# Empty expert slots left out of the gathers and stores of a mixture-of-experts block

## The chip, the cores and the metric

The kernel runs on one core of a Trainium2 chip. The metric is the device time of one execution in microseconds; the kernel before was timed in three runs.

## The reference

Two transformer blocks follow each other for 512 tokens of width 1024, in float32. The first has differential and latent attention, a cross attention to 256 memory tokens, and a mixture of 32 experts in 4 groups; the second has a gated delta rule, sliding-window attention and two feed-forwards. The change concerns the mixture alone, which for each token h is

```
g = top-1 group of softmax(h Wg + bg);  e1, e2 = top-2 experts of that group by softmax(h We + be)
w_k = p(g) * p(e_k) / (p(e1) + p(e2))
y = sum over k of w_k * (silu(h G[e_k]) * (h U[e_k])) D[e_k]      G, U: 1024 x 256,  D: 256 x 1024
```

The reference pads each expert's tokens to blocks and fills the rest with an empty token of weight 0.

## The kernel before

**Blocks and slots.** The kernel gives each expert a block of 64 slots (`SLOTS`). Experts 0 to 30 are the static blocks (`N_STATIC` = 31); expert 31, and what an expert has beyond 64 tokens, go into extra blocks, run by a loop whose count is read from the router's result. The router (`router_vector`, on DVE, with rank sums on PE) gives each of the 1024 pairs of token and choice a slot (`DEST`), and by a product of one-hot tables (`ids_tensor`) each slot its token (`IDS`). An empty slot gets the sum of nothing, token 0. A token's slots within a block are filled from slot 0 up.

**Rows in.** SP stores the tokens' rows (1028 floats with the norm's factor) to `rows_h` in DRAM. POOL gathers 128 of them for a pair of blocks by an indirect DMA (`gather`, L2269; the last pair and the extra block have 64), two buffers deep (`XB`); before the gather of pair q it waits until PE has turned pair q-2. DVE scales them, PE turns them (`turn_x`), DVE puts them into `XT` with the gain.

**Weights.** SP loads each block's weights as three pieces of 1 MB (`load_piece`, L1962, `load_extra`, L1976) into a ring of 16 places (`RING_X`) that borrow other tensors' memory. `queue` is their order, the order in which PE uses them; a piece is loaded when the piece 16 before it is done.

**Work.** `macros` is the order on PE, ACT and DVE: gate and up of block b (`gate_up`, L2011 and L2013), `down` of b-1 (L2022), the turn of b's hidden (L2097). The extra loop stands after down of block 23 (`X_AT` = 24), its result goes to buffer 0. In the first blocks and ahead of them PE also makes the second layer's memory keys (L2041).

**Rows out.** ACT copies the result [2 halves x 64 slots, 512] from PSUM to `YB` (in `scratch`, one buffer per parity, L2203) and itself issues two stores of 128 KB (`store_y`, L1984) to `rows_y`, which has a row for each slot; before it overwrites a buffer it waits for the stores of two blocks ago (`y_stored`). Slots of extra blocks that aren't run are filled with constants once, by a 4 MB DMA from POOL (L3527, `st_fill`).

**Combination.** When all stores have landed, POOL gathers for each of the four token tiles both choices' rows by slot (8 indirect DMAs, L2297). DVE adds them with their weights to `ROWS` (L2399), PE turns the sums back (L2357) and makes the beta products (L2342), ACT copies them to X, POOL multiplies by the final gain's row (L2304). SP meanwhile loads gdnin tiles of the second layer: six once the last pieces leave their places (`first_tiles`), the others as tiles are split.

## Time and profile before

| | |
|---|---|
| Median of three runs | 2062.88 us (2062.76 to 2064.25) |
| Span of the profiled execution | 2062.3 us |
| PE busy | 1919.4 us, 93% |
| DVE, ACT, POOL busy | 51%, 38%, 6% |
| DMA over the span | 261.07 MB, mean 127 GB/s |
| Expert stage, first gather to last gate and up | 463 to 726 us |

The profiled execution is told by its span alone; its own device time wasn't recorded, and the median stands 0.6 us above the span. A line of the trace names a place in the code (L2022), an engine and what it writes and reads by the program's names; PE is the matrix engine, PEld its weight load, SPq, ACTq and POOLq are the queues that issue DMAs. "<-" ahead of a name tells whose end released an instruction. The chain of waits is followed back from the last instruction. Each slice of the page is a fortieth of the span, 51.6 us.

### The profile page before, as it was taken

Reading aid. Unit: us, or ns where it says so; the run is one execution under the profiler, and the core shown is the slowest. Engines: PE = TensorE matmul, PEld = TensorE weight load, DVE = VectorE, ACT = ScalarE, POOL = GpSimd, SP = SyncE. Lnnn points to the kernel's source line nnn. Section 1 sums busy time; section 2 is a strip of 40 time slices with the busy share of each in tenths; the row PEclk is TensorE's granted clock in tenths of the full one; section 3 lists DMA queues with packets and bytes.
Section 4 is the critical chain, followed back from the end, with each engine's and each line's share of the span. In section 5 each row is a group of like instructions: output and inputs, shape, how many; then the busy total and the mean of one; then the engine's idle time right before and its main releaser. Section 6 shows DMA issues by size and latency. Waiting matters only on the chain.

```text
span 2062.3 us, 25543 instructions
## 1 busy us (share of the span) xinstructions
PE 1919.4 (93%) x9978; PEld 1494.5 (72%) x9978; DVE 1059.4 (51%) x1979; ACT 779.8 (38%) x1637; POOL 117.1 (6%) x85
## 2 busy tenths in 40 slices
PE   7999888998987759999898999999999999999997
PEld 5665567685544447788887888888876778888886
DVE  6757656352211147684554543644567754444344
ACT  4455744531111146533544331322345543222222
POOL 0000000000000034020420000000000000000000
PEclk9999989999999969999999999999999999999998
DMA  5101513449999951122001222222221022222221
GB/s 188 42 10 38 161 53 109 148 180 406 412 412 408 405 226 62 62 72 72 1 2 46 97 98 102 87 98 99 95 82 42 32 100 95 102 92 92 102 92 41
DMA packets 76792, 261.07 MB, mean 127 GB/s; under 512 B 7777, under 2 KB 10081, under 8 KB 76289
## 3 DMA queue, kind: packets, MB, share of 16 engines
q1 hardware_dynamic: 66512, 231.46, 30.7%
q0 software_dynamic: 5040, 19.58, 2.8%
q10 hardware_dynamic: 5120, 8.39, 1.1%
q8 instruction: 80, 1.31, 0.3%
q14 instruction: 40, 0.32, 0.1%
HBM read 242.62 MB, written 16.79 MB: 126 GB/s over the span
## 4 chain that ended last, share of the span: by engine, by line
PE 72%; DMA 7%; DVE 6%; ACT 3%; issue 1%; POOL 0%; SPq 0%; ACTq 0%; DVEq 0%; POOLq 0%
PE ps_pair L299 17%; PE ps_pair L300 17%; PE ps_pair L301 17%; PE ps_pair L2011 3%; DMA w_places<-w_experts 3%; DMA split_acts_as_f<-w_experts 3%; PE ps_turn L2576 2%; PE ps_pair L2576 1%; PE ps_pair L892 1%; PE ps_out L923 1%; PE ps_out L2022 1%; PE ps_turn L904 1%; PE ps_shared L2022 1%; PE ps_out L2342 1%; ACT g L3368 1%
## 5 line engine op out<-in xcount | busy, mean ns | idle before, releaser
L299 PE MATMUL ps_pair<-split_acts,w_high 128*128 128x512 f32 (+1 forms) x1816 | 723.2, 398 | 21.8 <-DVE split_acts L626 10.0
L301 PE MATMUL ps_pair<-split_acts,w_low 128*128 128x512 f32 (+1 forms) x1816 | 706.0, 389 | 0.0
L300 PE MATMUL ps_pair<-split_acts,w_high 128*128 128x512 f32 (+1 forms) x1800 | 700.0, 389 | 0.0
L299 PEld LDWEIGHTS ps_pair<-split_acts,w_high 128*128 128x128 f32 x1816 | 344.7, 190 | 103.2 <-issue 23.7
L242 DVE TENSOR_TENSOR w_low<-w_raw,w_high 128x1024 fp32r<-128x1024 f32 (+4 forms) x249 | 281.9, 1133 | 259.8 <-ACT w_high L236 257.8
L301 PEld LDWEIGHTS ps_pair<-split_acts,w_low 128*128 128x128 f32 x1816 | 344.2, 190 | 72.1
L300 PEld LDWEIGHTS ps_pair<-split_acts,w_high 128*128 128x128 f32 x1800 | 342.5, 190 | 67.6 <-issue 1.9
L236 ACT ACTIVATE w_high<-w_raw 128x1024 fp32r<-128x1024 f32 (+4 forms) x249 | 242.8, 976 | 147.2 <-PE ps_pair L301 143.2
L372 DVE TENSOR_TENSOR x<-x,ps_pair 128x512 f32<-128x512 f32 x80 | 54.9, 686 | 141.5 <-PE ps_pair L301 141.5
L2253 DVE TENSOR_TENSOR g<-g,ps_pair 64x256 f32<-64x256 f32 x31 | 13.2, 425 | 199.7 <-ACT g L2193 199.7
L3124 ACT ACTIVATE split_acts<-h 128x512 fp32r<-128x512 f32 x44 | 27.9, 633 | 200.2 <-DVE h L3137 200.2
L3119 ACT ACTIVATE h<-h 128x512 f32<-128x512 f32 x44 | 27.8, 632 | 138.4 <-DVE h L3130 138.3
L2011 PE MATMUL ps_pair<-split_acts_as_f 128*64 128x256 f32 x232 | 62.6, 426 | 16.4 <-DMA split_acts_as_f<-w_experts 10.8
L957 ACT ACTIVATE g<-ps_pair,columns 128x256 f32<-128x256 f32 (+3 forms) x112 | 57.4, 524 | 35.8 <-DVE columns L1011 33.9
L3134 DVE TENSOR_TENSOR h<-ps_pair,h 128x512 f32<-128x512 f32 x44 | 30.4, 691 | 78.5 <-PE ps_pair L301 78.5
L2013 PE MATMUL ps_pair<-split_acts_as_f 128*64 128x256 f32 x232 | 62.9, 427 | 0.0
L3130 DVE TENSOR_TENSOR h<-ps_pair,h 128x512 f32<-128x512 f32 x44 | 30.4, 691 | 58.9 <-PE ps_pair L301 53.2
L2576 PE MATMUL ps_turn<-split_acts_as_f 128*128 128x128 f32 x432 | 55.8, 280 | 3.9 <-ACT split_acts_as_f L2723 3.9
L2011 PEld LDWEIGHTS ps_pair<-split_acts_as_f 128*64 128x64 f32 x232 | 34.5, 153 | 33.4 <-issue 19.7
L2707 POOL TENSOR_TENSOR split_acts_as_f<-split_acts_as_f,consts 128x768 f32<-128x768 f32 x24 | 45.2, 1894 | 226.7 <-DVE split_acts_as_f L2692 131.5
L2576 PEld LDWEIGHTS ps_turn<-split_acts_as_f 128*128 128x128 f32 x432 | 52.9, 196 | 5.8 <-issue 5.0
L2193 ACT ACTIVATE g<-ps_pair 64x256 f32<-64x256 f32 x31 | 11.6, 375 | 120.0 <-PE ps_pair L2013 120.0
(528 smaller groups left out, 2459.1 us busy)
## 6 DMA issues: line engine op xcount, KB each, us to landing
w_raw<-w_gu SPq DMA_DIRECT2D x88, 512.0 KB, 3.4
split_acts_as_f<-w_experts SPq DMA_DIRECT2D x42, 1024.0 KB, 21.2
w_places<-w_experts SPq DMA_DIRECT2D x35, 1024.0 KB, 21.4
w_raw<-w_down SPq DMA_DIRECT2D x32, 448.0 KB, 3.2
w_raw<-w_gdnin SPq DMA_DIRECT2D x26, 512.0 KB, 3.4
w_raw<-w_out SPq DMA_DIRECT2D x24, 512.0 KB, 3.5
x<-w_experts SPq DMA_DIRECT2D x12, 1024.0 KB, 20.0
rows_y<-scratch ACTq DMA_DIRECT2D x64, 128.0 KB, 6.1
```

Source lines behind the costliest of these rows:

```text
L236: act.activation(WH[:, t % SPLIT, 0:kt * m], WRAW[:, t % RING, 0:kt * m], ACT.Copy).then_inc(high_ready, 1)
L242: dve.tensor_tensor(WL[:, t % SPLIT, 0:kt * m], WRAW[:, t % RING, 0:kt * m], WH[:, t % SPLIT, 0:kt * m].bitcast(F32), ALU.subtract).then_i ...
L299: pe.matmul(out, wh[:, k, :], self.high(k), start=(n == 0), stop=False)
L300: pe.matmul(out, wh[:, k, :], self.low(k), start=False, stop=False)
L301: last = pe.matmul(out, wl[:, k, :], self.high(k), start=False, stop=(n == self.kt - 1))
L372: dve.tensor_tensor(X[:, j, :], X[:, j, :], out, ALU.add).then_inc(evacuated[t % BANKS], 1)
L957: done(act.activation(self.member(self.prob(n), j, w), self.member(self.bank(m), j, w), ACT.Exp, bias=COL[:, c + j:c + j + 1], scale=self. ...
L2011: pe.matmul(out[rows, 0:256], xs, w[:, at_:at_ + 256], start=(k == 0), stop=(k == KT - 1), skip_group_check=True)
L2013: last = pe.matmul(out[high_rows, 0:256], xs, w[:, at_ + 256:at_ + 512], start=(k == 0), stop=(k == KT - 1), skip_group_check=True)
L2022: last = pe.matmul(out[n * SLOTS:(n + 1) * SLOTS, :], h[:, k * SLOTS:(k + 1) * SLOTS], w[:, k * 1024 + n * 512:k * 1024 + n * 512 + 512], ...
L2576: last = pe.matmul(pair(bank)[:, n, :], lhs(h), rhs(h), start=True, stop=True)
L2707: done(pool.tensor_tensor(CM[c], LT[c], wide(level(l)), ALU.mult), "c_pool", ("C", c, l))
```

## The change

Empty slots get indices out of bounds, and the indirect DMAs get a bound and skip them. Each slot's list entry now is 2 x token + choice - 1024 before the sum, so a filled slot gives 2 x token + choice, and an empty one 1024 (`OF_SLOT`); halved it is the token, or 512 where empty (`IDS`), and doubled plus the half (`HALF_ROWS`) it is the place of a half row of 512 floats in `rows_y`. `rows_y` shrinks from a row for each slot to 1024 rows in token order, both choices side by side. The gathers' bound is 511. Skipped rows keep what the buffer held, so POOL zeroes `XB` and `XE` once ahead of the first gather. The stores leave ACT's queue: POOL scatters the 128 half rows of a block with one indirect DMA (bound 2047). In the extra loop ACT waits for `e_free`, which POOL raises when the extra block's scatter has landed. The fill goes. At the end SP loads four token tiles, each both choices, with plain DMAs of 1 MB (`load_y`), in place of POOL's eight gathers.

```diff
+            by_choice = listed("tokens").rearrange("p (t k) -> p t k", k=2)
+            for k in range(2):
+                step(dve, dve.tensor_scalar(by_choice[:, :, k], col(C_TOKEN).to_broadcast([P, QT]), 2.0, float(k - 2 * S),
+                                            ALU.mult, ALU.add), "route_dve")
+                step(dve, dve.scalar_tensor_tensor(out=by_choice[:, :, k], in0=const("iota")[:, 0:QT], scalar=2.0 * P,
+                                                   in1=by_choice[:, :, k], op0=ALU.mult, op1=ALU.add), "route_dve", "lists")
...
                   ALU.is_equal))
-            by_tile = OF_BLK.rearrange("p (t k) b -> p t (k b)", k=2)
-            st(tt(by_tile, by_tile, wide(listed("tokens").unsqueeze(2), 2 * NB_MAX), ALU.mult))
+            st(tt(OF_BLK, OF_BLK, listed("tokens").unsqueeze(2).to_broadcast([P, 2 * QT, NB_MAX]), ALU.mult))
             st(tt(OF_ROW, places("rows", SLOTS), FROW.unsqueeze(2).to_broadcast([P, 2 * QT, SLOTS]), ALU.is_equal),
                "places")
             need(dve, "route_pe", "ids")
-            st(dve.tensor_copy(IDS[:, 0:15], ps_ranks[:, 256:271]), "ids")
-            st(dve.tensor_copy(IDS[0:SLOTS, 15:33], ps_ranks[0:SLOTS, 271:289]), "more ids")
+            st(ts(OF_SLOT, ps_ranks[:, 256:256 + NB_MAX], 2.0 * S, None, ALU.add), "more ids")
+            st(ts(IDS[SLOTS:P, 0:15], OF_SLOT[SLOTS:P, 33:48], 1, None, ALU.arith_shift_right))
+            st(ts(IDS[0:SLOTS, :], OF_SLOT[0:SLOTS, 0:33], 1, None, ALU.arith_shift_right), "ids")
+            in_half = CONST["band2"][0] + 7
+            st(ts(HALF_ROWS, OF_SLOT, 2.0, CB[:, in_half:in_half + 1], ALU.mult, ALU.add), "slots")
 
...
 
-        def store_y(act, b):
-            act.wait_ge(y_taken, b + 1)
-            for n in range(2):
-                act.dma_start(rows_y[b * SLOTS:(b + 1) * SLOTS, n * 512:(n + 1) * 512],
-                             YB[n * SLOTS:(n + 1) * SLOTS, b % 2, :]).then_inc(y_stored[b % 2], 16)
+        def scatter(pool, y, slots):
+            return pool.indirect_dma_start(out=rows_y.rearrange("r (n d) -> (r n) d", n=2),
+                                           out_offset=bass.IndirectOffsetOnAxis(ap=slots, axis=0), in_=y,
+                                           in_offset=None, bounds_check=4 * S - 1, oob_is_err=False)
+
+        def scatter_y(pool, b):
+            at_ = b // 2 if b % 2 == 0 else 33 + b // 2
+            pool.wait_ge(y_taken, b + 1)
+            scatter(pool, YB[:, b % 2, :], HALF_ROWS[:, at_:at_ + 1]).then_inc(y_stored[b % 2], 16)
 
...
                     load_piece(sp, r, extras)
+            return extras
+
+        def load_y(sp, extras):
+            for q in range(2):
+                sp.wait_ge(y_stored[q], 16 * ((N_STATIC + 1 - q) // 2))
+            sp.wait_ge(e_stored, 16 * extras)
+            for i in range(QT):
+                done(sp.dma_start(YGS(i), rows_y[2 * i * P:2 * (i + 1) * P, :].rearrange("(p k) d -> p (k d)", k=2)),
+                     f"ld_y{i}", by=16)
 
...
                     if b >= 2:
-                        act.wait_ge(y_stored[b % 2], 32 * (b // 2))
+                        act.wait_ge(y_stored[b % 2], 16 * (b // 2))
                     if b == X_AT:
-                        act.wait_ge(e_stored, 32 * extras + 32)
+                        act.wait_ge(e_free, extras + 1)
                     act.copy(YB[:, b % 2, :], ps_y[b % 2][:, :]).then_inc(y_taken, 1)
-                    store_y(act, b)
                     if b == 12:
                         final_row_scalar(act)
                 elif kind == "memory":
                     mem2_take(act, b)
                 else:
                     extras = n_extra(act)
-                    act.wait_ge(y_stored[0], 32 * (X_AT // 2))
-                    ev.wait(act, "st_fill", 16)
+                    act.wait_ge(y_stored[0], 16 * (X_AT // 2))
                     with act.Fori(0, extras) as j:
                         act.wait_ge(extra_free, 3 * j + 5)
                         act.activation(SG[0], ps_gu[0][rows, 0:256], ACT.Silu).then_inc(e_silu, 1)
                         act.wait_ge(e_h_turned, j + 1)
                         act.copy(HT[:, 0, :], ps_gu[0][:, 256:384]).then_inc(e_h_taken, 1)
                         act.wait_ge(extra_free, 3 * j + 6)
-                        act.wait_ge(e_stored, 32 * j + 32)
+                        act.wait_ge(e_free, j + 1)
                         act.copy(YB[:, 0, :], ps_y[0][:, :]).then_inc(e_taken, 1)
-                        act.wait_ge(e_taken, j + 2)
-                        for n in range(2):
-                            act.dma_start(rows_y[bass.ds((j + N_STATIC) * SLOTS, SLOTS), n * 512:(n + 1) * 512],
-                                          YB[n * SLOTS:(n + 1) * SLOTS, 0, :]).then_inc(e_stored, 16)
 
...
             return pool.indirect_dma_start(out=out, out_offset=None, in_=rows_h,
-                                           in_offset=bass.IndirectOffsetOnAxis(ap=ids, axis=0))
+                                           in_offset=bass.IndirectOffsetOnAxis(ap=ids, axis=0), bounds_check=S - 1,
+                                           oob_is_err=False)
+
+        def gather_pair(pool, q):
+            if q >= 2:
+                pool.wait_ge(x_turned, q - 1)
+            n = slice(0, min(P, (N_STATIC - 2 * q) * SLOTS))
+            gather(pool, XB[n, q % 2, :], IDS[n, q:q + 1]).then_inc(x_rows[q % 2], 16)
 
         def moe_gpsimd(pool):
+            need(pool, "rows_act", ("sq", 1, QT - 1))
+            done(pool.memset(XB, 0.0), "x_pool")
+            step(pool, pool.memset(XE, 0.0), "x_pool")
             need(pool, "route_dve", "ids")
             ev.wait(pool, "st_rows", 16 * QT)
-            for q in range(X_PAIRS):
-                if q >= 2:
-                    pool.wait_ge(x_turned, q - 1)
-                n = slice(0, min(P, (N_STATIC - 2 * q) * SLOTS))
-                gather(pool, XB[n, q % 2, :], IDS[n, q:q + 1]).then_inc(x_rows[q % 2], 16)
-                if q == X_AT // 2 + 1:
+            for q in range(3):
+                gather_pair(pool, q)
+            need(pool, "route_dve", "slots")
+            for kind, b in macros:
+                if kind == "gate":
+                    if b % 2 == 0 and b // 2 + 3 < X_PAIRS:
+                        gather_pair(pool, b // 2 + 3)
+                elif kind == "down" and b == X_AT - 1:
                     extras = n_extra(pool)
                     with pool.Fori(0, extras) as j:
                         pool.tensor_copy(ID_X, IDS[0:SLOTS, bass.ds(j + 16, 1)]).then_inc(e_ids, 1)
-                        pool.wait_ge(e_ids, j + 1)
+                        pool.wait_ge(e_ids, 2 * j + 1)
                         pool.sem_inc(x_go, 1)
                         gather(pool, XE, ID_X).then_inc(e_rows, 16)
+                        pool.tensor_copy(ID_Y, HALF_ROWS[:, bass.ds(j + 16, 1)]).then_inc(e_ids, 1)
+                        pool.wait_ge(e_ids, 2 * j + 2)
                         pool.wait_ge(e_turned, j + 1)
+                        pool.wait_ge(e_taken, j + 2)
                         pool.sem_inc(x_go, 1)
-            need(pool, "route_dve", "weights")
-            ev.wait(pool, "st_fill", 16)
-            for q in range(2):
-                pool.wait_ge(y_stored[q], 32 * ((N_STATIC + 1 - q) // 2))
-            pool.wait_ge(e_stored, 32 * extras + 32)
-            pool.sem_inc(x_go, 1)
-            for i in range(QT):
-                for q in range(2):
-                    done(pool.indirect_dma_start(
-                        out=YG(i, q), out_offset=None, in_=rows_y, in_offset=bass.IndirectOffsetOnAxis(
-                            ap=YIDX[:, 2 * i + q:2 * i + q + 1], axis=0), bounds_check=NB_MAX * SLOTS - 1),
-                        f"ld_y{i}{q}", by=16)
+                        scatter(pool, YB[:, 0, :], ID_Y).then_inc(e_stored, 16)
+                        pool.wait_ge(e_stored, 16 * j + 16)
+                        pool.sem_inc(e_free, 1)
+                    scatter_y(pool, b)
+                elif kind == "down":
+                    scatter_y(pool, b)
             need(pool, "row_act", 1)
...
                 load_piece(sp, r)
-            moe_sync(sp)
+            extras = moe_sync(sp)
             first_tiles(sp)
+            load_y(sp, extras)
             for t in range(MEMO_END + RING, N_TILES):
...
             done(pool.dma_start(raw1, a["mem_t"]), "ld_mem", by=16)
-            done(pool.dma_start(rows_y[N_EXPERTS * SLOTS:, :].rearrange("(n p) d -> p n d", p=SLOTS),
-                                CB[rows, 0:D].unsqueeze(1).to_broadcast([SLOTS, N_MORE - 1, D])), "st_fill", by=16)
             need(pool, *mla.last)
```

How this moves POOL's instructions. Before, from the first gather on to the loop over extra blocks (L2282; L1966 reads its count), POOL held only gathers, with the extra block's behind that of pair 13; two more followed, then the eight of L2297:

```order
L2269 DMA g<-rows_h,g_as_int 128x1028 [waits st_rows,route_dve]
L2269 DMA g<-rows_h,g_as_int 128x1028
L2269 DMA g<-rows_h,g_as_int 128x1028 [waits x_turned] x12
L1966 TENSOR_LOAD g_as_int [waits route_dve]
L1966 ISA x2
L2282 UNCONDITIONAL_BRANCH
L2282 ISA
L2283 COPY g_as_int<-g_as_int 64x1
L2284 REGISTER_ALU
L2269 DMA g<-rows_h,g_as_int 64x1028 [waits e_ids]
L2282 REGISTER_ALU [waits e_turned]
L2282 COMPARE_AND_BRANCH
```

With the change, the same loop (L2309), and what stands on both sides of it (L2284 gathers, L1990 scatters):

```order
L1990 DMA rows_y<-scratch,g_as_uint 2048x512 [waits y_taken] x2
L1974 TENSOR_LOAD g_as_int [waits route_dve]
L1974 ISA x2
L2309 UNCONDITIONAL_BRANCH
L2309 ISA
L2310 COPY g_as_int<-g_as_int 64x1
L2311 ISA
L2284 DMA g<-rows_h,g_as_int 64x1028 [waits e_ids]
L2314 ISA
L2314 COPY g_as_uint<-g_as_uint 128x1
L2315 REGISTER_ALU
```

Ahead of the loop now stand all scatters up to block 22 and the gathers up to pair 14; inside it, behind the gather, POOL waits for PE's turn (e_turned) and ACT's copy (e_taken) and scatters:

```order
L2316 REGISTER_ALU [waits e_ids]
L2317 REGISTER_ALU [waits e_turned]
L1990 DMA rows_y<-scratch,g_as_uint 2048x512 [waits e_taken]
L2320 ISA
L2309 REGISTER_ALU [waits e_stored]
L2309 COMPARE_AND_BRANCH
L1990 DMA rows_y<-scratch,g_as_uint 2048x512 [waits y_taken]
L2284 DMA g<-rows_h,g_as_int 64x1028 [waits x_turned]
L1990 DMA rows_y<-scratch,g_as_uint 2048x512 [waits y_taken] x7
```

Behind the loop follow the scatter of block 23, the last gather and seven scatters.

On SP, the end of the experts' weights (L1962 before, L1970 now) and the first gdnin tiles, before:

```order
L1962 DMA split_acts_as_f_51<-w_experts 128x2x1024 [waits piece_done] x2
L1962 DMA h<-w_experts 128x2x1024 [waits piece_done]
L1962 DMA split_acts_as_f_51<-w_experts 128x2x1024 [waits piece_done]
L3483 DMA w_raw<-w_gdnin 128x1024 [waits low_ready,piece_done] x6
L3483 DMA w_raw<-w_gdnin 128x1024 [waits low_ready] x20
```

and with the change:

```order
L1970 DMA split_acts_as_f_51<-w_experts 128x2x1024 [waits piece_done]
L3508 DMA w_raw<-w_gdnin 128x1024 [waits low_ready,piece_done] x6
L2011 REGISTER_ALU [waits y_stored1,y_stored0]
L2013 DMA split_acts_as_f_51<-rows_y 128x2048 [waits e_stored]
L2013 DMA split_acts_as_f_51<-rows_y 128x2048 x3
L3508 DMA w_raw<-w_gdnin 128x1024 [waits low_ready] x20
```

The four loads of L2013, and the waits for the scatters ahead of them, now stand between gdnin tiles 6 and 7.

## Rows read from the trace of the kernel before

**Rows 1.** The page's slices: the span in 40 equal parts.
```profile
DMA  5101513449999951122001222222221022222221
GB/s 188 42 10 38 161 53 109 148 180 406 412 412 408 405 226 62 62 72 72 1 2 46 97 98 102 87 98 99 95 82 42 32 100 95 102 92 92 102 92 41
```

**Rows 2.** Windows: busy time by engine, granted clock, DMA share, GB/s.
```profile
core 0: us, PE busy (x) PEld busy (x) DVE busy (x) ACT busy (x) POOL busy (x), PEclk, DMA share, GB/s
463.00:561.00 98.00, 92.56 (x624) 55.48 (x622) 22.43 (x45) 15.42 (x39) 8.11 (x9) 0.95 1.03 409
561.00:726.00 165.00, 131.74 (x900) 77.80 (x899) 26.59 (x47) 25.11 (x61) 7.65 (x9) 0.93 1.03 409
```

**Rows 3.** The chain of waits over 400 to 860 us: start, us, what.
```profile
561.75 21.44 DMA split_acts_as_f<-w_experts
...
706.25 19.57 DMA split_acts_as_f<-w_experts
```

**Rows 4.** DMA queues and issues, 463 to 726 us.
```profile
q1 hardware_dynamic: 23659, 91.23, 86.4%
q0 software_dynamic: 2320, 8.42, 8.3%
q10 hardware_dynamic: 4640, 7.61, 7.7%
...
rows_y<-scratch ACTq DMA_DIRECT2D x60, 128.0 KB, 6.1
```

**Rows 5.** The gathers of rows_h, line 2269: as a group, then POOL's timeline.
```profile
L2269 POOL DMA_INDIRECT g<-rows_h,g_as_int x17: 902/936/1022, 462.6 to 681.9; - x17
...
DMA to landing us min/median/max: 7.1/7.8/9.8
...
462.57 1.02 POOL L2269 DMA_INDIRECT g<-rows_h,g_as_int  x1 [145.36 <-DVE g_as_int L1852]
...
541.52 0.94 POOL L2269 DMA_INDIRECT g<-rows_h,g_as_int  x1 [11.41 <-PE ps_turn L2108]
...
617.32 0.94 POOL L2269 DMA_INDIRECT g<-rows_h,g_as_int  x1 [16.86 <-PE ps_turn L2108]
...
638.60 0.93 POOL L2269 DMA_INDIRECT g<-rows_h,g_as_int  x1 [0.80 <-POOL g_as_int L2283]
```

**Rows 6.** Timeline near the extra block and near block 30.
```profile
661.66 0.58 ACT L2203 COPY scratch<-ps_out 128x512 f32<-128x512 f32 x1 [1.34 <-PE ps_out L2022]
...
667.32 0.40 PE L2011 MATMUL ps_pair<-split_acts_as_f 128*64 128x256 f32 x1 [0.98 <-DVE split_acts_as_f L2263]
...
733.69 1.12 ACTq L1984 DMA_DIRECT2D rows_y<-scratch  x2
734.85 0.27 ACT L2196 COPY g<-ps_pair 128x128 f32<-128x128 f32 x1 [1.20 <-issue]
```

**Rows 7.** From the last copy to the sums: chain of waits, then timeline.
```profile
738.28 2.40 DMA rows_y<-scratch
...
743.76 6.51 DMA split_acts_as_f<-rows_y,g_as_uint
...
751.69 1.29 DVE g L2399
...
753.01 3.26 DVE g L2399
...
737.16 0.58 ACT L2203 COPY scratch<-ps_out 128x512 f32<-128x512 f32 x1 [2.04 <-PE ps_out L2022]
...
752.71 2.47 POOL L2304 TENSOR_TENSOR split_acts_as_f<-g,h 128x1024 f32<-128x1024 f32 x1
```

**Rows 8.** Single rows: weights' landing, the fill of rows_y, one small copy.
```profile
DMA to landing us min/median/max: 4.7/20.7/24.9
...
rows_y<-consts POOLq DMA_DIRECT2D x1, 4096.0 KB, 24.1
...
462.11 0.17 DVE L1851 CAST g_as_int<-ps_shared 128x15 int32<-128x15 f32 x1 [1.30 <-PE ps_shared L1773]
```

More of the change, by code:

```diff
@@ L77 @@
 _w = 0
-for _n, _k in (("rows", SLOTS), ("blocks", NB_MAX), ("tokens", QT), ("down4", N_GROUPS), ("down8", PER_GROUP),
+for _n, _k in (("rows", SLOTS), ("blocks", NB_MAX), ("tokens", 2 * QT), ("down4", N_GROUPS), ("down8", PER_GROUP),
                ("first_slot", N_EXPERTS), ("extra_slot", N_EXPERTS)):
@@ L1701, in make_lists @@
                     (blocks[:, 0:even], even, 2.0, 0.0), (blocks[:, even:NB_MAX - odd], N_MORE, 1.0, float(N_STATIC)),
[L1702 removed]
+                    (blocks[:, NB_MAX - odd:], odd, 2.0, 1.0),
                     (listed("down4"), N_GROUPS, -1.0, float(N_GROUPS)),
@@ L1770, in ids_tensor @@
             for c in range(2 * QT):
-                pe.matmul(ps_ranks[0:SLOTS, 256:289], OF_ROW[:, c, :], OF_BLK[:, c, 0:33], start=(c == 0),
-                          stop=(c == 2 * QT - 1), skip_group_check=True)
-                last = pe.matmul(ps_ranks[SLOTS:P, 256:271], OF_ROW[:, c, :], OF_BLK[:, c, 33:48], start=(c == 0),
-                                 stop=(c == 2 * QT - 1), skip_group_check=True)
+                for half in (slice(0, SLOTS), slice(SLOTS, P)):
+                    last = pe.matmul(ps_ranks[half, 256:256 + NB_MAX], OF_ROW[:, c, :], OF_BLK[:, c, :], start=(c == 0),
+                                     stop=(c == 2 * QT - 1), skip_group_check=True)
             done(last, "route_pe", "ids")
@@ L2188, in moe_scalar @@
             act.sem_inc(e_taken, 1)
-            act.sem_inc(e_stored, 32)
+            act.sem_inc(e_free, 1)
             for kind, b in macros:
```

15 lines of the change are left out of this document (8 added, 7 removed).

## Prediction

> **What bounds the kernel now.** I read the page's slices first, to find the stage, then the windows over that stage, the chain of waits through it, the DMA queues of the same stretch, and last the timeline of its end.
>
> The slices [rows 1] put the experts into slices 9 to 13, where the DMA digit is 9 and the rate stands at 405 to 412 GB/s; nowhere else does it stay there. The windows [rows 2] split the stage. From 463 to 561 us PE is busy 92.56 of 98 us; from 561 to 726 us it is busy 131.74 of 165, so it idles 33.3 us. In both the DMA share is 1.03 at 409 GB/s: the engines are full for all 263 us. The chain [rows 3] agrees: from 561.75 us it steps from one landing of expert weights to the next, each some 21 us after its issue, until 725.82 us, when gate and up of block 30 can start. So **the number of bytes moved up to 725.82 us sets that moment**, and PE only follows. The queue table of this stretch [rows 4] says whose bytes they are: the weights (q1) hold 86.4% of the engines' time, the row gathers (q0) 8.3% with 8.42 MB, the stores of the results (q10) 7.7% with 7.61 MB.
>
> **The change, part by part.**
>
> *Bytes left out.* The 17 gathers [rows 5] fetch 15 x 128 + 2 x 64 = 2048 slots of 4112 B, which is the 8.42 MB. Only 1024 slots are filled: 512 tokens with 2 experts each. (The reference's router on its own inputs gives the experts 18 to 46 rows, mean 32, none over 64, so the loop over extra blocks runs once, for expert 31.) If an index out of bounds moves nothing, half of q0 and q10 goes: (8.42 + 7.61) / 2 = 8.02 MB, at 409 GB/s **19.6 us**. By engine time it is (8.3% + 7.7%) / 2 of 263 us = 21.0 us; I use 19.6. PE doesn't forbid it, with 33.3 us idle behind the transfers.
>
> But a piece of weights counts as landed only when all 16 engines have brought their share, and the empty slots are always the high ones of a block. If an engine carries neighbouring rows, those with low slots keep their load and hold back every piece. No row of before shows which row goes over which engine, so this is bounded: 0 us if one engine carries only slots that are always filled (each expert has at least 18), 19.6 us if the empty ones spread evenly. I take the middle, **9.8 us**: a block has 64 slots and a mean of 32 filled, so some unevenness is sure, and one engine keeping all its load is the extreme.
>
> The Trainium skill (DMA: Bandwidth & Descriptors, "The descriptor swizzle") says of a plain 128-partition transfer that engine 0 has partitions 0 to 3 and 32 to 35, engine 1 the next four of each, and so on, with engines 8 to 15 on the upper 64. If indirect DMAs follow this, the most loaded engine would, by the experts' counts, lose some 10 us of work up to the last piece; no row here shows it, and the sum doesn't use it.
>
> *Start of the stage.* Before the first gather DVE now makes three small copies for two; one costs 0.17 us [rows 8]. The two MEMSETs of POOL wait for the last square and have until 462.57 us, when POOL ends an idle time of 145.36 us [rows 5]. They write 2056 and 1028 columns; the nearest POOL row, 128x1024 in 2.47 us [rows 7], bounds them at 7.5 us together, and the DVE chain that they stand beside takes from 446 to 462 us. Even if this moved the first gather by 1 us, the queues hold work then (share 1.03). **0.**
>
> *The removed fill of rows_y* (4 MB at 213 us, 24.1 us to landing [rows 8]): it is done by 237 us, nobody waits for it before the extra block, and no DMA stands in the chain of those 40 us. **0.**
>
> *POOL's queue.* It now scatters: 32 more indirect DMAs of about 0.94 us [rows 5], 30 us in 270, beside 16 us of gathers. Gather q+3 stands ahead of the scatters of two blocks, at the place where PE's transposes release it, as before. Per block POOL works 1.4 us of 8.9. **0**, while the scatters' landing fits, see the last rival.
>
> *The extra block.* Before, XE's gather was issued at 638.60 us right behind a pair's gather [rows 5]. Now it stands behind the scatter of block 22 (copied out at 662.24), so it lands near 662.2 + 0.9 + 1 (counter and copy) + 0.9 + 7.8 (the median landing of a gather) = 672.8, and after scaling and turning (2 us) its gate starts some 8 us later than at 667.32 [rows 6]. POOL then waits for that result, scatters it, waits for its landing, and only then sends block 23's rows; behind it stand gather 15 and all later scatters, and ACT waits for e_free before it overwrites the buffer with block 24. The cover: PE needs about 6.2 us per block, the transfers 8.9, so blocks 24 to 30 hold 7 x 2.7 = 19 us to catch up, or 14 us if all bytes vanish. Gather 15 isn't wanted before the gate of 28. **0**, and if that cover were gone, up to 8 us.
>
> *The stores leave ACT's queue.* ACT had copied block 29 out, then from 733.69 issued two stores, and only then copied the turned hidden of block 30, for which PE waited [rows 6]: 734.85 - 733.69 = **1.2 us** off the path.
>
> *From the last result to the combination* [rows 7]. Before, counted from the end of the last copy (737.75): store landed at 740.68, POOL's two first gathers until 743.76, landing at 750.27, and the sum of token tile 1 ready at 756.27, which is 18.5. From there PE's own transposes and beta products set the pace. Now: scatter issue 0.95, landing between 2.4 (store, idle queues) and 7.8 (gather, full queues), SP's issue 0.5, a plain 1 MB load 4.7 (the shortest landing of a 1 MB piece [rows 8]), two sums of 1.29, then tile 1's two sums, one of them stretched to 3.26 by POOL's product that runs beside it. With 2.4, since the six gdnin tiles have landed by then: 0.95 + 2.4 + 0.5 + 4.7 + 2.6 + 4.6 and 0.1 for the wake-ups between = 15.9, and 2.6 are gained; with 7.8 it is 2.8 lost. The four loads also stand ahead of gdnin tiles 7 and 8 on SP; those are first needed after 775 us. I take **2.6 us**.
>
> Sum: 9.8 + 1.2 + 2.6 = 13.6 us off. The profiled span is 2062.3 us, the median of the three runs 2062.88; the 0.6 between lies around the span and stays. **2062.9 - 13.6 = 2049.3 us.**
>
> **Rivals.**
>
> *All of it comes.* The rows that are skipped spread evenly over the engines: 19.6 + 3.8 = 23.4 us, **2039.5 us**. For it: the gathers of 64 rows and of 128 share the same queues and nothing in the page shows an engine behind the others. Against it: filled slots are neighbours.
>
> *The transfers aren't relieved.* Either a skipped index still moves a packet of the same length, or one engine carries only low slots. Then only the end gains: **2059.1 us**, just inside 0.2% of before. For it: no operation of before is bounded, so nothing shows that skipping saves engine time.
>
> *Slower: the scatters land late.* ACT may overwrite a result buffer only when the scatter of two blocks ago has landed, so two blocks can't take less than copy 0.6 + issue 1.0 + landing. Two blocks take 12.35 us early (0.94 + 11.41 from gather to gather before the one at 541.52) and 17.8 later (0.94 + 16.86 before 617.32) [rows 5]. The loop decides once a landing passes 10.8 us early, 16.2 late. With 18 us, 15.5 pairs take 304 us where 263 are taken now, so 41 - 4 = 37 us more: **2100 us**. For it: weights take 21 us to land in these queues. Against it: gathers from the same software queue land in 7.1 to 9.8, stores in 6.1.
>
> **How the numbers follow.** Forecast 0.47, all of it 0.26, no relief 0.20, late scatters 0.07. The range of 8 in 10 must hold the first three with the tail's bounds: from 2037 (all, by engine time, and 1 us more at the end) to 2062 (no relief, and the scatter before the combination landing late). The forecast's own range is 2043 to 2056. What a measurement of this kernel can tell from no change is about 0.2%, 4.1 us: faster is under 2058.8. Forecast and all of it lie there, of no relief a third: 0.47 + 0.26 + 0.07 = 0.80. Same: 0.13. Slower: 0.07.
>
> **What would show it.** Right: over the stage q0 and q10 together shrink to about half their bytes (q10 gone); the last piece of weights lands 8 to 12 us earlier; DMA share stays near 1.03 up to it, or falls below 1 while pieces still take as long, which would be idle engines waiting for a loaded one. PE's idle time in the stage shrinks by the same amount. From the last copy to the first transposes of tile 1 some 16 us instead of 18.5. Wrong: landings of weights as late as before with half the bytes gone (no relief), a landing 19 us earlier (even spread), ACT or PE waiting for y_stored (late scatters), or a gap on PE at the extra block that reaches block 30.

## The result, and the profile after

The changed kernel takes **2043.4 us** (median of 4 runs, 2042.07 to 2046.95), beside 2062.82 us for the kernel before on the same chip: ratio 0.9905, 95% interval 0.9893 to 0.9917. That is 19.4 us less, where 13.6 were forecast (2049.3 us, range 2037 to 2062). The direction and the range held; the size lies between the forecast and the rival "all of it comes" (2039.5). Measured again in two further groups (e5 and e12 below), the changed kernel gave 2044.14 and 2044.56 us. So two medians of one kernel differ by up to 1.2 us, and the interval of each ratio is some 2.5 to 3 us to either side.

The page of the changed kernel, its slices and queues over the span:

```profile
DMA  5101213449999931121002222232321033222221
GB/s 190 43 10 40 78 50 110 154 173 398 409 409 405 397 129 64 61 73 62 1 1 68 93 96 100 88 109 89 97 83 42 23 103 103 97 94 92 99 93 41
...
q1 hardware_dynamic: 67088, 235.65, 32.4%
q0 software_dynamic: 5408, 11.19, 1.6%
```

The plateau of 9s is as high as in [rows 1] and ends in slice 14, where 226 GB/s have become 129: the stage is as full as before, and shorter. The windows, over the same first stretch and then up to block 30's last products:

```profile
463.00:561.00 98.00, 92.29 (x648) 54.28 (x646) 20.48 (x35) 15.53 (x41) 18.54 (x18) 0.97 1.02 404
561.00:711.00 150.00, 126.78 (x884) 72.67 (x885) 26.25 (x46) 22.46 (x58) 27.51 (x29) 0.92 1.03 406
```

Against [rows 2], the DMA share (last but one column) is still 1.02 to 1.03, and PE idles 23.2 us in the second stretch where it idled 33.3. The queues of 463 to 711 us:

```profile
DMA packets 28608, 100.43 MB, mean 405 GB/s; under 512 B 4126, under 2 KB 4126, under 8 KB 28592
...
q1 hardware_dynamic: 23941, 92.17, 93.4%
q0 software_dynamic: 4651, 8.03, 8.7%
...
rows_y<-scratch,g_as_uint POOLq DMA_INDIRECT x30, 6.1
g<-rows_h,g_as_int POOLq DMA_INDIRECT x15, 7.3
```

Against [rows 4], q10 is gone and q0 holds gathers and scatters together in 8.03 MB, where the two queues had 16.03 MB. The scatters land in 6.1 us, as the stores did.

The chain of waits through the stage and behind it:

```profile
459.60 7.58 DMA g<-rows_h,g_as_int
...
613.23 19.80 DMA w_places<-w_experts
...
650.33 6.33 DMA g<-rows_h,g_as_int
...
679.75 20.16 DMA x<-w_experts
...
716.80 0.71 issue
717.51 4.09 DMA rows_y<-scratch,g_as_uint
...
721.71 4.81 DMA split_acts_as_f<-rows_y
...
726.63 1.29 DVE g L2424
727.95 1.30 DVE g L2424
729.27 1.30 DVE g L2424
730.59 3.27 DVE g L2424
```

Weights still set the pace, but the extra block's gather now stands in the chain too, and the last steps can be set beside [rows 7].

**One subtraction first.** Not all of the 22.0 us between the two profiled spans (2062.3 and 2040.3) belongs to the change. The chains of before and of the changed kernel, at one and the same instruction (the copy of the turned logits, far from any edit):

```profile
444.23 1.37 ACT g L1745 x5
```

```profile
440.17 1.37 ACT g L1753 x5
```

4.1 us are there before the router has even run, in code that is the same in both. Most of them stand beside a lower granted clock of TensorE in the profile of before. The window of 415 to 420 us (PEclk is the third column from the end), before and then in the changed kernel:

```profile
415.00:420.00 5.00, 5.00 (x21) 4.09 (x20) 2.31 (x13) 0.00 (x0) 0.00 (x0) 0.66 0.61 213
```

```profile
415.00:420.00 5.00, 5.00 (x31) 4.32 (x30) 1.89 (x4) 0.78 (x2) 0.00 (x0) 1.00 0.57 196
```

The lag grows by 1.6 us there, and by 1.6 us at 150 to 165 us, where the clock was 0.89 and 1.00. The three profiles of the changed kernel (this one, e5, e12) agree within 1.0 us at the copy, but those of edited versions of it reach it up to 4.4 us later (e6), and e3, with the same instructions up to there, 1.4 later. Over 405 to 415 us, just ahead of the dip, PE was busy 6.2 of 10 us in before and 8.4 in the changed kernel; why the profiles differ there isn't shown. I therefore count shifts from that copy on: −4.9 at the first block's copy to `YB`, −21.0 at the last block's, −22.4 at the first product of the second layer's gated delta rule (774.94 before, 752.53 now). So of the profile 0.9 us fall to the first gather and turn, **16.1 to the blocks, 1.4 to the way from the last copy to the sums**: 18.4 together, beside 19.4 by the medians.

The blocks' 16.1 us are not all the transfers' either. From the first gather to the landing of the last piece that gate and up of block 30 need pass 263.3 us before (462.57 to 725.82) and 248.2 now (459.60 to 707.8 by the piece's semaphore): 15.1 us less. From that landing to the end of the last copy pass 11.9 and 8.9 us. Of these 3.0 us, 1.3 belong to ACT's queue (below) and some 1.7 stand beside the granted clock over block 30, before and now:

```profile
726.00:738.00 12.00, 9.24 (x51) 5.02 (x51) 0.42 (x1) 1.81 (x4) 0.00 (x0) 0.86 0.91 361
```

```profile
705.00:717.00 12.00, 9.98 (x65) 4.93 (x61) 0.85 (x2) 3.10 (x8) 1.94 (x2) 1.00 0.80 321
```

### The profile page after: what moved, and what is told of

It reads as the page before. It is cut to its first block, busy times and chain, and to the rows that moved or that the text cites. A ratio compares the mean times of both kernels' runs of the same rounds, so it can differ in the third digit from the quotient of the medians.

```text
span 2040.3 us, 25547 instructions
## 1 busy us (share of the span) xinstructions
PE 1910.2 (94%) x9978; PEld 1485.6 (73%) x9978; DVE 1060.0 (52%) x1983; ACT 777.7 (38%) x1637; POOL 145.0 (7%) x111
## 4 chain that ended last, share of the span: by engine, by line
PE 74%; DVE 7%; DMA 4%; ACT 4%; issue 1%; SPq 0%; POOL 0%; DVEq 0%; POOLq 0%; ACTq 0%
PE ps_pair L299 18%; PE ps_pair L300 17%; PE ps_pair L301 17%; PE ps_pair L2032 4%; PE ps_turn L2601 2%; DMA w_places<-w_experts 2%; PE ps_pair L2601 1%; PE ps_pair L892 1%; PE ps_out L2043 1%; DMA x<-w_experts 1%; PE ps_out L923 1%; PE ps_shared L2043 1%; PE ps_turn L904 1%; DMA g<-rows_h,g_as_int 1%; PE ps_out L2367 1%
## 5 line engine op out<-in xcount | busy, mean ns | idle before, releaser
L299 PE MATMUL ps_pair<-split_acts,w_high 128*128 128x512 f32 (+1 forms) x1816 | 721.6, 397 | 21.5 <-DVE split_acts L626 9.4
L2268 DVE TENSOR_TENSOR g<-g,ps_pair 64x256 f32<-64x256 f32 x31 | 13.2, 424 | 175.5 <-ACT g L2214 175.5
L2032 PE MATMUL ps_pair<-split_acts_as_f 128*64 128x256 f32 x232 | 59.1, 408 | 6.6 <-DMA w_places<-w_experts 3.1
L2034 PE MATMUL ps_pair<-split_acts_as_f 128*64 128x256 f32 x232 | 59.3, 408 | 0.0
L620 ACT ACTIVATE split_acts<-x,vectors 128x512 fp32r<-128x512 f32 x40 | 28.1, 721 | 73.5 <-DVE x L372 71.3
```

The source lines that it names most:

```text
L299: pe.matmul(out, wh[:, k, :], self.high(k), start=(n == 0), stop=False)
L2032: pe.matmul(out[rows, 0:256], xs, w[:, at_:at_ + 256], start=(k == 0), stop=(k == KT - 1), skip_group_check=True)
L2034: last = pe.matmul(out[high_rows, 0:256], xs, w[:, at_ + 256:at_ + 512], start=(k == 0), stop=(k == KT - 1), skip_group_check=True)
```

## The experiments

Two theories stood after this. **A**: the saving is nearly that of the bytes (19.6 us), since the skipped rows relieve all 16 DMA engines to much the same degree. **B**: it is that of the slowest engine (0 to 19.6 with the layout), and the rest of the 19.4 came from elsewhere: the fill, the extra block, the tail. All ratios are to the kernel before in the same group.

The last two columns come from one profiled execution of each run. "Stage" is the time from the start of the first gather to the landing of the last piece for gate and up of block 30; it leaves out what happens ahead of the stage and behind it, and the three profiles of the changed kernel agree in it within 0.6 us. Each piece of weights raises its semaphore 16 times; "spread" is the time from the first of these to the last for that same piece.

| run | us (range) | ratio, 95% | stage, us | spread, us |
|---|---|---|---|---|
| before | 2062.82 (2062.75 to 2064.25) | | 263.3 | 5.1 |
| changed kernel | 2043.40 (2042.07 to 2046.95) | 0.9905 [0.9893, 0.9917] | 248.2 | 12.1 |
| e1_spread | 2041.15 (2039.19 to 2043.81) | 0.9897 [0.9881, 0.9912] | 243.5 | 5.2 |
| e2_packed | 2056.34 (2052.94 to 2057.99) | 0.9968 [0.9957, 0.9979] | 257.6 | 12.3 |
| e3_extra_early | 2046.03 (2043.16 to 2047.28) | 0.9920 [0.9906, 0.9933] | 249.0 | 11.9 |
| e4_spread_extra | 2042.43 (2041.23 to 2043.33) | 0.9901 [0.9886, 0.9917] | 244.2 | 5.4 |
| e5_again (changed kernel) | 2044.14 (2041.98 to 2044.68) | 0.9907 [0.9892, 0.9922] | 248.1 | 12.1 |
| e6_read_all | 2053.86 (2048.97 to 2054.50) | 0.9943 [0.9929, 0.9956] | 254.2 | 7.6 |
| e7_write_all | 2051.90 (2049.77 to 2054.40) | 0.9946 [0.9932, 0.9960] | 252.3 | 8.7 |
| e8_both_all | 2060.79 (2058.46 to 2064.64) | 0.9987 [0.9978, 0.9996] | 261.4 | 3.9 |
| e9_fill | 2045.53 (2040.46 to 2051.61) | 0.9919 [0.9905, 0.9934] | 248.4 | 12.2 |
| e10_product_late | 2043.39 (2042.23 to 2044.71) | 0.9908 [0.9894, 0.9923] | 248.4 | 11.9 |
| e11_spread_late | 2037.81 (2035.72 to 2038.42) | 0.9878 [0.9863, 0.9892] | 244.5 | 5.7 |
| e12_base (changed kernel) | 2044.56 (2041.22 to 2046.72) | 0.9911 [0.9898, 0.9923] | 248.7 | 12.0 |

### Which rows are empty: e1_spread and e2_packed

Both only permute the slots of a block over the partitions, in the router's list of places; all experts compute what they did. With a = half of 32 partitions, e = 0 to 7, d = 0 to 3, partition 32a + 4e + d gets slot e + 8d + 32a in e1 and 8e + 4a + d in e2 (by default it has slot 32a + 4e + d):

```diff
+            for a_ in range(2):
+                part = listed("rows")[:, 32 * a_:32 * a_ + 32].rearrange("p (e d) -> p e d", d=4)
+                step(dve, dve.tensor_scalar(part, const("iota")[:, 0:4].unsqueeze(1).to_broadcast([P, 8, 4]), 8.0,
+                                            32.0 * a_, ALU.mult, ALU.add), "route_dve")
+                step(dve, dve.scalar_tensor_tensor(out=part, in0=const("iota")[:, 0:8].unsqueeze(2).to_broadcast([P, 8, 4]),
+                                                   scalar=1.0, in1=part, op0=ALU.mult, op1=ALU.add), "route_dve", "lists")
```

(e2 has 1.0, 4.0 * a_ and 8.0 for the three factors.) If an engine has four neighbouring partitions of each 32, e1 gives every engine the same share of filled rows and e2 gives some engines only filled ones.

> The changed kernel with another order of the slots within a block: row p of a block (p = 32a + 4e + d) holds slot 32a + e + 8d, so that the filled slots lie spread over the block's 64 rows. Nothing else differs, the bytes are the same. Theory 'uneven engines' (each DMA engine serves neighbouring rows, so engines with low slots keep more of their load and every piece of weights waits for them): the slowest engine now saves as much as the mean, the last piece lands 4 to 7 us earlier, the spread of a piece's 16 landings falls from 12 us back to the 3 to 5 us of the kernel before, time 2037 to 2039 us. Rival 'engines are dealt rows evenly' (the skew has another source): no change, 2043 us within 2.

> The changed kernel with the filled slots packed: row p = 32a + 4e + d holds slot 8e + 4a + d. Theory 'uneven engines': an engine that serves rows 4e to 4e+3 and 32+4e to 32+4e+3 now has slots 8e to 8e+7, so the engine with slots 0 to 7 saves nothing from skipping (every expert has at least 18 rows): the transfers are as long as in the kernel before and 11 to 14 us longer than in the changed kernel, time 2054 to 2058 us. If engines take 8 rows in a row instead (8e to 8e+7), this order is the even one and the time falls by 4 us or more. Rival 'dealt evenly': 2043 us within 2.

Measured: e2 is 12.9 us slower than the changed kernel (2056.34 beside 2043.40), with the same rows and bytes, inside its expected range. e1 is 2.3 us faster, which is less than was expected and, by the medians alone, within the intervals. The stage tells more: 243.5 us for 248.2, 4.7 less, where one kernel repeats within 0.6; and in e4 beside e3 and e11 beside e10, the same pair of layouts, it is 4.8 and 3.9 us less, the medians 3.6 and 5.6. The last step of the weights in the chains of e1 and of e2, which end at 705.4 and 721.6 us:

```profile
686.00 19.39 DMA split_acts_as_f<-w_experts
```

```profile
701.95 19.61 DMA split_acts_as_f<-w_experts
```

So the layout decides, and the engines can be seen where the transfers end. The DMA rows of a window of 60 us (40 slices of 1.5 us each) over that moment, before:

```profile
DMA  9999999999999942706899999998000000000000
GB/s 401 415 412 399 410 417 419 415 404 421 412 412 404 337 173 87 164 0 208 227 341 336 404 401 418 426 399 330 22 0 0 0 0 0 0 0 5 0 0 0
```

The changed kernel:

```profile
DMA  9999999999997753120659999999600000000000
GB/s 415 407 410 421 418 388 385 410 412 412 399 380 322 284 205 150 55 104 19 76 229 431 421 426 437 437 391 415 243 0 0 0 0 0 0 0 0 0 0 0
```

e1_spread:

```profile
DMA  9999999999999998407999999990000000000000
GB/s 404 415 407 410 415 404 408 408 410 412 407 418 410 388 373 344 163 0 175 431 415 431 431 421 431 396 363 11 0 0 0 0 0 0 0 0 0 0 0 0
```

e2_packed:

```profile
DMA  9999999999984333433047999999950000000000
GB/s 369 415 366 418 377 412 398 392 391 415 407 322 197 161 153 158 161 159 137 27 55 306 431 431 410 421 426 418 410 199 0 0 0 0 0 0 0 0 0 0
```

The first run of 9s is the end of the weights and the first gdnin tiles; the second is what is loaded for the combination. What tells is how the first one ends (slices counted from 0). Before, and in e1, the rate falls from about 400 to under 180 within two to four slices. In the changed kernel it takes from slice 12 to slice 18: the engines finish one after the other over some 9 us. In e2 there are 7 slices with three or four tenths busy: that is the share of about 6 of 16 engines, for some 10 us, when the others have nothing left. Earlier in e2's stage the rate is lower too, as it would be if the others stood idle at times:

```profile
DMA packets 16478, 57.94 MB, mean 386 GB/s; under 512 B 2354, under 2 KB 2354, under 8 KB 16469
```

over 561 to 711 us, where the changed kernel has 406 in the windows above. The semaphores' spreads in the table say the same (in e2 up to 16.6 us, at 572 us).

e1 gains 5.6 us within the blocks (shift from first to last copy 21.7 instead of 16.1) but reaches the first gather 2.3 us later (461.90 beside 459.60 us). This isn't the work of its four added steps on DVE: from the end of the turned logits' copy to the first gather pass 18.1 us in both, and in e11. The 2.3 us are there ahead of the copy, 1.6 of them at 415 us, where e1's granted clock is 0.71; e3, which hasn't these steps, has 0.80 there and the same loss.

### Where the saving is: e6_read_all, e7_write_all, e8_both_all

e6 gives the gathers a bound of 512 and one more row, so empty slots fetch a row again; e7 gives each empty slot a half row of its own behind the token rows, so the scatters write all 128. e8 does both. No result depends on what they add.

```diff
-        rows_h = nc.dram_tensor("rows_h", [S, ROW_W], F32).ap()
-        rows_y = nc.dram_tensor("rows_y", [2 * S, D], F32).ap()
+        rows_h = nc.dram_tensor("rows_h", [S + 1, ROW_W], F32).ap()
+        rows_y = nc.dram_tensor("rows_y", [2 * S + 64 * NB_MAX + 1, D], F32).ap()
...
-            st(ts(HALF_ROWS, OF_SLOT, 2.0, CB[:, in_half:in_half + 1], ALU.mult, ALU.add), "slots")
+            APART = AF[:, 30, 0:NB_MAX]
+            st(ts(APART, const("iota")[:, 0:NB_MAX], float(P), col(C_TOKEN), ALU.mult, ALU.add))
+            st(dve.scalar_tensor_tensor(out=APART, in0=OF_SLOT, scalar=2.0 * S, in1=APART, op0=ALU.is_ge,
+                                        op1=ALU.mult))
+            st(dve.scalar_tensor_tensor(out=APART, in0=OF_SLOT, scalar=2.0, in1=APART, op0=ALU.mult, op1=ALU.add))
+            st(ts(HALF_ROWS, APART, 1.0, CB[:, in_half:in_half + 1], ALU.mult, ALU.add), "slots")
```

> The changed kernel, but the gathers of x move every slot again: rows_h has one row more, and the bound lets the empty slots' index (512) through, so they all fetch that row, as the kernel before fetched token 0. The scatters still skip. Theory 'slowest engine': an engine that serves slots 0 to 3 and 32 to 35 saves 23 to 36% of the gathers' 20 us, so this costs 4 to 7 us: 2047 to 2050 us. Rival 'bytes alone' (the mean engine sets the pace): half of the gathers' 20 us, 10 us: 2053 us.

> The changed kernel, but the scatters write every half row again: the empty slots' half rows go to places of their own behind the 1024 rows of rows_y, 2 KB each. The gathers still skip. Theory 'slowest engine': the stores' load on the engine with the low slots returns by 30% of 21 us: 5 to 7 us slower than e5_again, 2048 to 2051 us. Rival 'bytes alone': 9 to 10 us slower, 2053 us.

> Both edits together: no byte is saved, what is left of the change is POOL's scatters for ACT's stores, the plain loads at the combination and the missing fill. If the two costs add and the transfers set the pace: e5_again plus both single costs, 2055 to 2060 us, 3 to 6 us under the kernel before (ACT's queue 1.2, the combination 1.4 to 2.6). Rival 'the form counts' (scatters cost more or less engine time than the stores they replace): under 2053 us or over 2063 us.

Measured beside e5_again: +9.7, +7.8, together +16.7 us by the medians. The parts sum to 17.5, and e8, 0.8 us above its expected range, is left with 2.8 us of gain over before, which is all the change brings without its bytes. The stage columns give less: +6.1, +4.2, together +13.3 us. The last step of the weights in e8's chain ends at 725.3 us, 261.4 behind its first gather:

```profile
705.69 19.57 DMA split_acts_as_f<-w_experts
```

Counted from the turned logits' copy to the first product of the gated delta rule, e8's profile is 14.1 us slower than e5's and 4.4 faster than before. Most of what the medians have more isn't in the stage: in the profiles e5 reaches that copy at 441.9 us, e6 and e8 at 445.9 and 445.7, like the kernel before (445.6), again beside lower clocks (0.67 and 0.66 over 415 to 420 us). **So the bytes left out brought 13 to 17 of the 19.4 us**, 13.3 by the stage and 16.7 by the medians, against 9.8 in the prediction.

In the stage the two costs don't add: 6.1 + 4.2 is 3.0 us short of 13.3. With one kind skipped the spread is 7.6 or 8.7 us, between the 3.9 of e8 and the 12.1 of the changed kernel, so each half of the change brings unevenness of its own. By that measure e6 and e7 lie at what the theory of the slowest engine expected (4 to 7, 5 to 7), by the medians at or 1 to 2 us under what the rival expected (10, 9 to 10): these two runs don't decide between the theories. And e8's stage is 1.9 us shorter than that of before with the same 16.03 MB: by the packet records of 463 to 700 us its scatters take 2.44 us of the mean engine's time per MB where the stores before take 2.60, which for 7.61 MB makes an estimate of 1.2 us.

### Is the extra block covered: e3_extra_early, e4_spread_extra

The extra block's gather moves up to the gate of block 20, into its own buffer. In the loop, behind the extra block's turn, stands the gather for a next extra block (here an empty one). e4 has e1's layout as well.

```diff
+                    if b == X_AT - 4:
+                        extras = n_extra(pool)
+                        gather_extra(IDS[0:SLOTS, 16:17], 1)
...
-                        gather(pool, XE, ID_X).then_inc(e_rows, 16)
...
+                        gather_extra(IDS_MORE[0:SLOTS, bass.ds(j + 17, 1)], 2 * j + 3)
```

> The changed kernel, but POOL fetches the extra block's rows at the gate of block 20, four blocks ahead, in place of behind the scatter of block 22. Theory 'covered' (the gap on PE at the extra block is caught up by block 30, since the transfers set the pace): block 24's result comes some 7 us earlier, the last one and the time don't move (within 1 us of the changed kernel). Rival 'the gap reaches the end' (POOL's chain at the extra block also delays the scatters and what waits for them): 3 to 7 us faster.

> Both edits of e1_spread and e3_extra_early. Theory: with even engines the transfers end earlier, so PE has less time to catch up behind the extra block: 0 to 3 us faster than e1_spread. If e1_spread gains nothing, this equals e3_extra_early.

The wait the edit removes is real. In the changed kernel, waits of 640 to 665 us and POOL's timeline:

```profile
PE ps_turn L2191 <- DVE g L2242: 8.0, 1, 8.0
```

```profile
650.33 1.00 POOL L2284 DMA_INDIRECT g<-rows_h,g_as_int  x1 [0.90 <-issue]
```

In e3 the gather goes out at 627.61 us and PE's wait of 8.0 us is gone (the shift at the 25th copy, the extra block's, is −9.8 us, where the changed kernel has −5.8). Yet the time is 2046.03 us beside 2043.40, and e4's is 2042.43 beside e1's 2041.15: no gain where within 1 us was expected of e3 and a gain of 0 to 3 of e4, but 2.6 and 1.3 us more, by medians whose intervals overlap, and the stages are 0.8 and 0.7 us longer. In the changed kernel catching up takes until about block 29: behind the gap PE runs from 666.9 to 698.1 us without a pause over 0.1 us and then waits 2.0 us for weights again. The cover held, and was nearly used up.

### The fill: e9_fill

```diff
+            ev.wait(pool, "st_fill", 16)
...
+            done(pool.dma_start(rows_y.rearrange("(n p) d -> p n d", p=SLOTS),
+                                CB[rows, 0:D].unsqueeze(1).to_broadcast([SLOTS, N_MORE - 1, D])), "st_fill", by=16)
```

> The changed kernel with the fill of the y rows back at its old place (one store of 4 MB of zeros on ACT's queue in layer 0's late tiles, and GpSimd's wait for it ahead of the first gather). Theory (the fill lay beside work that TensorE bounds, its removal is worth nothing): no difference within 0.7 us of the changed kernel in the same group, about 2043 to 2044.5. Rival (part of the change's gain is the fill's): its 4.19 MB at the pace of full engines, some 10 us, or at least 2 to 3 us slower, 2046 or more.

(The store stands on GpSimd's queue, as in the kernel before, not on ACT's as the expectation has it.) Measured 2045.53 beside 2044.56 us, 1.0 apart with intervals that overlap widely. The profiled executions settle it better: both spans are 2042.7 us, the two stand within 0.5 us of each other at 28 of the 32 blocks' copies, the last among them, and the stages are 248.4 and 248.7 us. The fill is worth nothing that shows here, and the rival is out.

### The tail: e10_product_late, e11_spread_late, e12_base

```diff
-                need(pool, "comb_dve", ("sum", i))
+                need(pool, "comb_dve", ("sum", min(i + 1, QT - 1)))
```

> The changed kernel with one order at the combination changed: GpSimd's product of token tile i waits until VectorE's sum of the next tile (at most tile 3) has been made. Theory A: in the profiles VectorE's sum of tile 1 takes 3.27 us where the others take 1.3, because GpSimd computes at the same time; without that neighbour it takes 1.3 and the tail is 2 us shorter, about 2041.5. Theory B: GpSimd's product is needed just behind the sum, so what VectorE gains the products lose: within 0.5 us of the changed kernel, or 1 us slower. Neither expects anything to move ahead of the combination.

> Both edits together: the slots of each block spread over the partitions so that the filled rows fall evenly on the DMA engines, and the products at the combination moved later. If the two are independent (one acts in the stage of the experts, the other behind it): the changed kernel less 2 to 2.5 us for the spread and less 2 us for the products, about 2039.5. If the products' order is worth nothing: about 2041.

> The changed kernel, word for word, as the base of this group: 2043 to 2044.5, ratio 0.9905 within 0.0010. It tells how far two measurements of one kernel lie apart, which is the bound for reading the other three.

The chain of e10 shows the mechanism of theory A:

```profile
730.25 1.30 DVE g L2424
...
731.57 1.30 DVE g L2424
...
732.91 1.97 PE ps_turn L2382 x8
```

The sum that took 3.27 us beside POOL's product takes 1.30 without it. From the end of the last copy (717.74) to tile 1's transposes pass 15.2 us; in the changed kernel 17.2. But the time is 2043.39 us beside 2044.56, of 2.0 us only 1.2 at most, and that is within the intervals. In the profile the 2.0 us are there up to the first product of the gated delta rule, but POOL's first product now comes 2.6 us later behind the last copy, and by ACT's first write of `h` behind the products, at 760 us, 1.2 us are left. Theory A is right on the cause and wrong on the price.

e11 is **the fastest kernel here, 2037.81 us**, 6.7 us under e12, more than the 4 to 4.5 expected. Its stage is 4.2 us shorter, and from the last copy to the first product of the gated delta rule it takes 2.3 us less (33.4 for 35.7). Not all that the profiles differ by is the edits' doing. Of their 6.8 us, 4.3 have come by that product, since e11 began the stage 2.1 us later; 1.2 more arise over 750 to 760 us, where the granted clock is 0.92 in e11 and 0.58 in e12, and 1.4 in

```profile
860.00:880.00 20.00, 17.34 (x89) 14.86 (x88) 17.28 (x20) 5.64 (x11) 6.68 (x3) 0.91 0.17 53
```

where e12 shows a clock of 0.91 and the earlier profile of the same changed kernel 1.00. I read 4 to 6.5 us as gained by the two edits.

## Why the prediction was right, and where it was wrong

**"The number of bytes moved up to 725.82 us sets that moment"**: right. With the bytes back (e8) the stage is back to within 1.9 us of before and the time to within 2.8, with nothing else undone.

**"If an index out of bounds moves nothing"**: right in bytes (q0 8.03 MB for what was 16.03). A skipped row isn't quite nothing: in a gather it leaves a packet of 4 bytes, and in a scatter two skipped half rows leave one of 8, 9 ns each in the packet records, where a packet of 4096 bytes takes 159. That is why 4126 packets are "under 512 B" in the queue rows, where before has 2588 over its stage. (The prediction's reason for doubt, "no operation of before is bounded", is wrong: the eight gathers of the combination, L2297, have a bound. But they move all 1024 rows (4.19 MB), so they show nothing of skipping.)

**"I take the middle, 9.8 us"**: the step that failed, a term of the sum that was too small. It measured 13.3 us by the stage, 16.7 by the medians. The frame of 0 to 19.6 us was sound, and the layouts nearly reach both its ends: less the 1.9 us that e8's stage keeps, the bytes bring 17.9 us in e1's stage, 13.2 in the changed kernel's and 3.8 in e2's (by the medians, less 2.8: 18.6, 16.6 and 3.4). What was wrong was to take the middle, with "some unevenness is sure" as the only reason. Unevenness is there (landings spread over 12 us instead of 5) and costs 4 to 5 us of the stage, not 9.8. The account of bytes has the same size: up to the piece for block 30 the weights' queue has moved 132.9 MB since the program's start in the changed kernel, 131.1 in e1, 131.6 before. The 1.9 MB more than in e1 are what the lightly loaded engines had brought ahead of need, 4.6 us at 406 GB/s. SP has issued pieces ahead (16 places in the ring), so an engine with fewer rows goes on with the next piece and the DMA share stays at 1.03; only in e2 did the rate fall through the stage (386 GB/s).

The Trainium skill (DMA: Bandwidth & Descriptors, "The descriptor swizzle") gives engine 0 the partitions 0 to 3 and 32 to 35, and so on. Layouts chosen by that rule did what it says, e2 worse by 12.9 us and e1 more even, so the runs agree with it for indirect DMAs too. The estimate worked out from it, that the most loaded engine loses some 10 us of work, was 3 us short by the stage and over 6 by the medians: how the heavily loaded engine gets more relief than its own rows give isn't shown, since the records don't name a packet's engine. It stays open.

**"Start of the stage: 0"**: 1.1 us in fact, and covered. The MEMSETs took 1.81 and 0.95 us, not 7.5, and stand at 441.59 us beside the router. The first gather goes out 1.1 us later behind the router than before (behind the start of DVE's first small copy 1.5 us for 0.5), but its rows come soon enough that the first block's copy is 0.9 us earlier.

**"The removed fill: 0"**: right (e9). **"POOL's queue: 0"**: right, a scatter takes 0.97 to 1.04 us of POOL, and its landing, 6.1 us, is far from the 10.8 from which late scatters would decide.

**"The extra block: its gate starts some 8 us later"**: right in size (PE waited 8.0 us), and "0" was right for the sum (e3).

**"The stores leave ACT's queue, 1.2 us"**: right. PE's wait for the turned hidden of block 30, before and after:

```profile
735.17 1.94 PE L2022 MATMUL ps_out<-split_acts_as_f,g 128*64 128x512 f32 x8 [1.87 <-ACT g L2196]
```

```profile
714.17 1.94 PE L2043 MATMUL ps_out<-split_acts_as_f,g 128*64 128x512 f32 x8 [0.58 <-ACT g L2217]
```

1.87 − 0.58 = 1.3 us.

**"From the last result to the combination, 2.6 us"**: too large, 1.4 measured. The scatter landed in 4.09 us, not the 2.4 taken: it goes out at 717.5 us while the queues are still draining (the GB/s rows above). In e3, where it is issued into emptier queues, it took

```profile
721.34 2.41 DMA rows_y<-scratch,g_as_uint
```

The rest is as predicted: loads 4.81 for 4.7, sums 1.3, the stretched one 3.27.

Sum by the profiles, from the turned logits' copy: stage 15.1 (13.3 the bytes, the rest the scatters' form), ACT's queue 1.3, the clock over block 30 some 1.7, the combination 1.4, less 1.1 for the later first gather, is 18.4 us. Forecast were 9.8 + 1.2 + 2.6 = 13.6. So the time came within the range with the mechanism right, its largest term too small, and some 3.5 us from two things that the sum didn't have: the scatters' form, and the granted clock over block 30. Whether that clock is luck of the two executions or comes of PE's shorter waits (2.6 us for weights just before block 30's gate in before, 0.6 now) isn't shown.

## What to carry to other kernels

Where transfers set the pace and loads are issued many pieces ahead, bytes left out can come close to their full share even if they fall somewhat unevenly on the DMA engines: here the ordinary layout lost 4 to 5 us of 18, but the packed one lost 14. A middle between two bounds is no estimate: ask for the load of the most loaded engine, and test it with a layout that evens it out. Where a list decides which partitions are empty, the order in the list is a lever of its own: here 15 us lie between the best and the worst. And when the change is 1% of the time, measure the stage as well as the whole: the stage repeated within 0.6 us, the medians within 1.2.

## What the hardware showed that was not expected

- The same number of rows skipped by the same instructions cost 2041.2 or 2056.3 us, by the partitions they fall on.
- In the scatters' packet records two half rows of 2 KB that both go out share one packet of 4096 bytes and 159 ns, where the plain stores before took a packet of 2048 bytes and 84 ns for each. Per MB that is 2.44 us of the mean engine for 2.60.
- VectorE's sum of 128x1024 takes 1.30 us alone and 3.27 us when GpSimd starts a product of the same size beside it.
- Profiled executions differ in code that no edit touches, with different granted clocks in the same place: by 4.1 us ahead of the router between before and the changed kernel (0.66 and 1.00 at 415 to 420 us), and by 2.6 us between two profiles of the changed kernel behind the stage (0.91 and 1.00 at 860 to 880 us). A comparison of two profiles has to begin where the edit begins.
